# Token shift of the first two tiles moved into the projection's last chunks, and the leading tile's identity products taken out, in a hybrid RWKV-7 and latent-attention encoder step

## What is computed

```python
def _project(xn, shift_prev, w_in, mu_shift):
    p = jnp.einsum('bld,dc->blc', xn, w_in)
    pr, pm = p[..., :C_RWKV], p[..., C_RWKV:]
    prev = jnp.concatenate([shift_prev.astype(pr.dtype), pr[:, :-1]], axis=1)
    return pr + mu_shift * (prev - pr), pm, pr[:, -1:]
```

## Time and profile before

| | us |
|---|---|
| median of three runs | 2065.2 (2061.5 to 2069.67) |
| the profiled execution | 2070.0 |
| its span, first to last instruction | 2067.8 |
| projection, to the last copy by ACT | 308.9 |
| first instructions of the mixing of the prompt | 311.5 |
| PE busy in the span | 1895.7 |
| mean granted PE clock | 0.949 |

### The profile page before, as it was taken

The page is one execution under the profiler, slowest core; times in us unless marked ns, Lnnn a source line. Parts: engine busy times, 40 slices in busy tenths (PEclk is TensorE's granted clock), DMA queues, the critical chain, the costliest instruction groups (busy, mean ns, idle before and its releaser), DMA issues. The chain is left out here.

```text
span 2067.8 us, 39290 instructions
## 1 busy us (share of the span) xinstructions
PE 1895.7 (92%) x16543; PEld 1621.1 (78%) x16543; DVE 934.5 (45%) x1810; ACT 670.2 (32%) x1318; POOL 356.3 (17%) x330
## 2 busy tenths in 40 slices
PE   6999995888898898898877999999999999999997
PEld 6999993666666666666665888999999999899996
DVE  7610105455666655655425365333354333543335
ACT  2221211234344444444323113333343333333332
POOL 0000004322322221221110041300003100032100
PEclk9999996779999999999788999999999999999999
DMA  6452111101210110100133514444434444444441
GB/s 223 139 202 68 65 44 54 47 5 45 77 40 21 58 58 2 57 33 26 52 99 135 193 52 121 129 126 122 126 119 151 138 127 122 123 142 141 127 128 61
DMA packets 167889, 196.28 MB, mean 95 GB/s; under 512 B 18786, under 2 KB 142458, under 8 KB 166580
## 3 DMA queue, kind: packets, MB, share of 16 engines
q1 hardware_dynamic: 165556, 186.35, 28.7%
q0 software_dynamic: 2192, 7.93, 1.0%
HBM read 165.82 MB, written 29.25 MB: 94 GB/s over the span
## 5 line engine op out<-in xcount | busy, mean ns | idle before, releaser
L675 DVE TENSOR_TENSOR c_wo_lo<-c_raw,c_wo_hi 128x1024 fp32r<-128x1024 f32 x94 | 115.2, 1225 | 454.9 <-ACT c_wo_hi L602 454.7
L821 PE MATMUL c_pY<-c_wo_hi,c_hl 128*128 128x512 f32 x564 | 221.3, 392 | 0.0
L821 PE MATMUL c_pY<-c_wo_lo,c_hh 128*128 128x512 f32 x564 | 221.0, 392 | 0.0
L821 PE MATMUL c_pY<-c_wo_hi,c_hh 128*128 128x512 f32 x564 | 220.5, 391 | 0.0
L602 ACT ACTIVATE c_wo_hi<-c_raw 128x1024 fp32r<-128x1024 f32 x94 | 99.7, 1061 | 325.0 <-PE c_pY L821 325.0
L562 POOL TENSOR_TENSOR c_hid<-c_relu 128x384 f32<-128x384 f32 x96 | 79.3, 826 | 669.7 <-ACT c_relu L617 669.7
L853 PE MATMUL c_pU<-c_zT_hi,c_wo_hi 128*128 128x384 f32 x768 | 151.3, 338 | 1.7 <-DVE c_zT_lo L670 1.6
L853 PE MATMUL c_pU<-c_zT_lo,c_wo_hi 128*128 128x384 f32 x768 | 148.6, 334 | 0.0
L853 PE MATMUL c_pU<-c_zT_hi,c_wo_lo 128*128 128x384 f32 x768 | 148.5, 334 | 0.0
L853 PEld LDWEIGHTS c_pU<-c_zT_hi,c_wo_hi 128*128 128x128 f32 x768 | 137.7, 188 | 10.2 <-DVE c_zT_lo L670 2.7
L853 PEld LDWEIGHTS c_pU<-c_zT_hi,c_wo_lo 128*128 128x128 f32 x768 | 134.5, 188 | 0.0
(11 more groups left out here) (463 smaller groups left out, 3444.8 us busy)
## 6 DMA issues: line engine op xcount, KB each, us to landing
c_raw<-w_down SPq DMA_DIRECT2D x96, 512.0 KB, 3.6
c_raw<-w_up SPq DMA_DIRECT2D x96, 512.0 KB, 4.7
scratch_p<-a_o SPq DMA_DIRECT2D x72, 154.0 KB, 1.8
a_w<-w_in SPq DMA_DIRECT2D x8, 1232.0 KB, 8.3
m_prev<-scratch_p SPq DMA_DIRECT2D x8, 896.0 KB, 4.6
m_pr<-scratch_p SPq DMA_DIRECT2D x5, 1232.0 KB, 5.3
b_pr<-scratch_p SPq DMA_DIRECT2D x4, 1232.0 KB, 5.3
scratch_h<-a_x POOLq DMA_DIRECT2D x9, 512.0 KB, 4.5
```

The lines of the kernel that those rows point to most:

```text
L675: dve.tensor_tensor(row_lo[slot_of(U)], row_raw[U % 2][:, :], row_hi[slot_of(U)].bitcast(F32), ALU.subtract).then_inc(S("row_lo"), 1)
L821: last = pe.matmul(pY[2 * t + half][:, :], x, w[:, 512 * half:512 * half + 512], start=first and a == 0, stop=final and a == 2, skip_group ...
```

## The change

1. In the projection's last pair the SP loads, as soon as chunk 5 is stored in full, the first 1792 columns of tile 0 and of the rows one earlier, and some six tiles later those of tile 1. DVE, behind its last `w_low`, does the shift of both tiles in three operations each. Chunk 7 takes the meta tile and tile 1 first, and SP then loads their other 672 columns. To hold the rows across the barrier, `w_raw` is laid over the two `pr` buffers, and the input ring with `ln_in_g` and `ln_in_b` becomes a tensor `ring` that later phases use for other buffers.
2. `shift_diff` and `shift` of tiles 0 and 1 are gone from the mixing, with the loads of `pr` and `prev` for them and the waits on them. SP no longer waits for tile 0's transposes before it loads tile 1's table.
3. The constants that DVE sets move from the head of the phase to tile 0's `latent_keys`, POOL's two clears to its `lora_up`, behind `key_squares`.
4. All seven groups of identity products in tile 0 are gone.

```diff
-        x = [sb(f"a_x{i}", [P, D]) for i in range(RING)]
-        g_row, b_row = sb("a_g", [P, D]), sb("a_b", [P, D])
+        x = [M["ring"][:, i, :] for i in range(RING)]
+        g_row, b_row = M["ring"][:, 4, :], M["ring"][:, 5, :]
+
+        rows_early = [M["pr0"], M["pr"]]
+        past_early = [M["ring"][:, 2 * i:2 * i + 2, :].rearrange("p a d -> p (a d)") for i in range(EARLY)]
...
-        w_raw = [sb(f"a_w{i}", [P, KD, CH]) for i in range(2)]
+        w_raw = [rows_early[i][:, :].rearrange("p (k n) -> p k n", k=KD) for i in range(2)]
...
+        def tiles_of(half, more):
+
+            return list(range(NW)) if more or half == 0 else [NW - 1] + list(range(NW - 1))
...
+                    for m, w in enumerate(tiles_of(half, more)):
+                        if not more and (half, m) in ((0, 0), (1, EARLY)):
+                            for slot in range(4):
+                                sp.wait_ge(S(f"p_stored{slot}"), 16 * ((c + half) * NW + m) // 4)
+                        if not more and (half, m) == (0, 0):
+                            load_shifted(0)
+                        if not more and (half, m) == (0, 6):
+                            load_shifted(1)
+                        if not more and (half, m) == (1, EARLY):
+                            for i in range(EARLY):
+                                t0, n = TILES[i]
+                                sp.dma_start(rows_early[i][0:n, C_RWKV:C_IN], io["p"][1 + t0:1 + t0 + n, C_RWKV:C_IN])\
+                                  .then_inc(S("rest_landed"), 16)
+                        store_p((c + half) * NW + m, c + half, (NW * half + m) % 4, w)
+
+            def load_shifted(i):
+
+                t0, n = TILES[i]
+                if i == 0:
+                    sp.wait_ge(S("h_transposed"), 2 * NW)
+                    for s in range(RING):
+                        sp.wait_ge(S(f"h_stored{s}"), 16 * len(range(s, NW, RING)))
+                sp.wait_ge(S("w_lo"), N_CH - 1 + i)
+                sp.dma_start(rows_early[i][0:n, 0:C_RWKV], io["p"][1 + t0:1 + t0 + n, 0:C_RWKV])\
+                  .then_inc(S(f"early_landed{i}"), 16)
+                sp.dma_start(past_early[i][0:n, 0:C_RWKV], io["p"][t0:t0 + n, 0:C_RWKV]).then_inc(S(f"early_landed{i}"), 16)
...
+            dve.wait_ge(S("weights_landed"), 16 * len(mix_loads(io, M)))
+            for i in range(EARLY):
+                n = TILES[i][1]
+                p_, past = rows_early[i][0:n, 0:C_RWKV], past_early[i][0:n, 0:C_RWKV]
+                dve.wait_ge(S(f"early_landed{i}"), 32)
+                step(dve.tensor_tensor(past, past, p_, ALU.subtract))
+                step(dve.tensor_tensor(past, past, M["mu"][0:n, :], ALU.mult))
+                step(dve.tensor_tensor(p_, p_, past, ALU.add))
...
-    return steps
+    return [(s, i, v) for s, i, v in steps if i >= EARLY or s not in ("shift_diff", "shift")]
...
-                if i == 0 and step in ("newton_x", "scan_sa", "scan_s"):
-                    spin(pe, SC[:, 0:P], ident, ident, 12 if (step, v) == ("newton_x", 0) else 3)
...
-                    if i == 0:
-                        pe.wait_ge(S("sh_mu"), 1)
-                        spin(pe, SC[:, 0:512], ident, four_const, 3)
...
-                    if i == 0:
-                        spin(pe, SC[:, 0:P], ident, ident, 16)
...
+                if s == "lora_up" and i == 0:
+                    pool.memset(vbd[:, :], 0.0).then_inc(S("vbd_zero"), 1)
+                    pool.wait_ge(S("vbd_zero"), 1)
+                    pool.memset(kTall[QH:QH + 1, :, :], 0.0).then_inc(S("later_clear"), 1)
+                    pool.wait_ge(S("later_clear"), 1)
...
                 if s == "key_squares":
-                    pool.wait_ge(S("shifted"), i + 1)
+                    wait_shifted(pool, i)
+                    if i == 1:
+                        pool.wait_ge(S("KT_src"), 1)
+                        pool.wait_ge(S("b_ready"), 1)
...
                 if s == "decay":
+                    if i == 1:
+                        J.wait_filled(act, (0, "KT"))
+                        act.wait_ge(S("BT_src"), 1)
...
+                if s == "latent_keys" and i == 0:
+                    dve.memset(qT[QH:QH + 1, :, 0:CHUNK], -1e30).then_inc(S("first_set"), 1)
+                    dve.memset(qT[QH:QH + 1, :, CHUNK:P], 0.0).then_inc(S("first_set"), 1)
+                    for m in (CM, QM, PM):
+                        step(dve.memset(m, 0.0))
+                    for m in (IA, X0):
+                        for ck in range(2):
+                            R = rows_of(P, ck)
+                            step(dve.tensor_copy(m[R, :, :], ident[R, R].unsqueeze(1).to_broadcast([CHUNK, HEADS, CHUNK])))
+                    dve.memset(state[:, :, :], 0.0).then_inc(S("state_ready"), 1)
```

More of the change, by code:

```diff
@@ L101 @@
 N_CH = C_IN // CH
+EARLY = 2
 ORDER = list(range(1, LAST + 1)) + [0]
@@ L254, in pair @@
                 for half in range(2):
-                    for w in range(NW):
-                        u = NW * half + w
-                        drain((c + half) * NW + w, u % 4, w, c * 4 * NW + 16 * (u // 4))
-                        if w == 1 and (half == 0 or more):
+                    for m, w in enumerate(tiles_of(half, more)):
+                        u = NW * half + m
+                        drain((c + half) * NW + m, u % 4, w, c * 4 * NW + 16 * (u // 4))
+                        if m == 1 and (half == 0 or more):
                             w_high(c + half + 1, 1 - half)
@@ L363, in project, with pair @@
                 last.then_inc(S("p_filled"), 1)
-            def pair(c):
+            def pair(c, more):
                 for half in range(2):
                     pe.wait_ge(S("w_lo"), c + half + 1)
-                    for w in range(NW):
-                        pe.wait_ge(S("p_drained"), (c + half) * NW + w - 3)
-                        project((NW * half + w) % 4, half, w)
+                    for m, w in enumerate(tiles_of(half, more)):
+                        pe.wait_ge(S("p_drained"), (c + half) * NW + m - 3)
+                        project((NW * half + m) % 4, half, w)
             pe.wait_ge(S("ident_landed"), 16)
@@ L386, in _ @@
             with pe.Fori(1, N_CH // 2 - 1) as j:
-                pair(2 * j)
-            pair(N_CH - 2)
+                pair(2 * j, True)
+            pair(N_CH - 2, False)
 BLK = 3
```

75 lines of the change are left out of this document (35 added, 40 removed).

## The result

| | before | after |
|---|---|---|
| median of the runs taken together, us | 2064.69 (4 runs, 2061.5 to 2069.67) | 2037.13 (4 runs, 2033.83 to 2038.1) |
| the profiled execution | 2070.0 | 2037.2 |
| its span | 2067.8 | 2035.4 |
| PE busy in the span | 1895.7 | 1879.3 |
| mean granted PE clock | 0.949 | 0.950 |

The ratio is 0.9861, 95% interval 0.9842 to 0.9879: 27.6 us faster, where 26.4 were forecast.

What follows compares the result with a forecast made beforehand. It took PE to bound the projection and a chain beside PE the mixing's first 22 us. 16.5 − 3.5 + 5.4 + 2.4 + 1.8 + 3.6 + 1.0 − 0.8 = 26.4 us, giving 2039; range 2031 to 2047.

Steps and rivals of the forecast that it cites:

- both of tile 1: Tile 1's shift leaving the mixing gains 3.6 us; its norm, no longer held beside POOL's key product, gains 1.0.
- the constants: Constants and clears inside tile 0's chain hold the key norm and delay the key copy: 3.5 us lost, bounds 0 and 4.6.
- identity products: Removing tile 0's groups gains 5.4 us in the Gram products, 2.4 before the first X, 1.8 in later steps.
- What bounds: PE bounds the projection; a chain beside PE (constants, shift, norm) bounds the first 22 us of the mixing.
- that case, with 2.7: If the rotation table lands some 1.5 us earlier, POOL's clear ends earlier and the constants lose 2.7 us.
- the last: Three products each ahead of the third X product, scan_sa and scan_s: removal gains 1.8 us, bounds 0 and 5.0.
- The first rival: The clock stays low through tile 1's wide products, up to 11.5 us more, 2050; 12 in 100.
- The term of 0.8: Lower granted clock without the identity products: 0.8 us lost, bounds a gain of 1 and a loss of 6.
- Given back: The start's gain is lost to something the shift hid, such as a longer load: 2051 to 2057; 6 in 100.
- slower: SP's waits and loads in the projection make PE stand still over 26 us, ending above 2065.2; 3 in 100.
- More: No hold, an early table, all identity groups worth full time: 35.8 us gained, 2029 to 2031; 7 in 100.

Runs made afterwards that it cites:

- e9: The changed kernel with 8 more DVE subtractions of 128x1792 behind the early shift in the projection; median 2048.25 us, ratio to before 0.9883.
- e10: The changed kernel with 24 more DVE subtractions of 128x1792 behind the early shift in the projection; median 2054.36 us, ratio to before 0.9914.
- e6: The changed kernel with POOL's clear of the key tile's last row moved behind tile 1's key product; median 2041.19 us, ratio to before 0.9869.
- e2: The changed kernel with all seven groups of identity products back at their old places; median 2048.95 us, ratio to before 0.9885.
- e8: The changed kernel with POOL's clear and DVE's memsets moved, and identity products added while PE awaits tile 0's latent row; 2039.35 us, ratio 0.9868.

## Why the prediction was right

The forecast was 2039, and 2037.1 and 2043.9 were measured, 27.6 and 23.5 us less than before on the same chips. The mechanism is borne out by the terms: four of eight, among them both of tile 1, came out within 0.1 us. That the sum fell within 0.3 us is luck: the constants gave 2.0 us more than forecast, and three other terms 1.7 less. And two terms that look right hide errors of their own, as told under identity products.

- **What bounds.** The start was a chain beside PE; e9 shows that the work moved into the projection is free, and e10 that its cover is DVE's idle time up to the barrier.
- **The constants** were mis-sized, −3.5 against −1.5. The mechanism was right: the clear holds a one-input `TENSOR_SCALAR` until its own end (e6: 0.16 without it). The rule of the Trainium skill, page "SBUF — State Buffer", section "Who interferes with whom", said that the clear, which reads nothing, would block such an operation and not a two-input one; the trace agrees with both: L1855 at 2.25 us, and L1839, with two tensor inputs beside the same clear, at 0.47 as before. What was off is the moment: the table landed 1.5 us after its issue and not 3.6, so the clear ended at 323.47 instead of 325.6, and the block of constants ended 2 us sooner. The prediction named that case, with 2.7; the rest is that the latent row, from which this term counts, came 0.5 later than put. So the copy stood at 333.93, where PE's products at half clock would have released it at 332.5; e6 gets 1.3 us back by moving the clear.
- **Identity products**: 9.6 forecast, 8.3 between the traces of before and after, 9.2 by putting them back. The step that was wrong is the last, and not by its 1.8 being too high: the three places cost 3.0 (e2), each 1.65 us of products of which 0.7 to 1.1 reached the chain. The prediction took the clock of before there to be the lower level, from the stretch of 385.3 to 392.0; but right ahead of it, from 381.9 to 385.3, PE ran at 0.99. That is 2.2 us of clock that the changed kernel lacks and the sum does not have, so that only 0.8 is left to see.
- **The clock.** The first rival is refuted: tile 1's key, value and query products ran at 1.00 from 366.6 to 378.0, though the stretch ahead of them, 350.5 to 364.0, was at 0.50 with PE busy 12.32 of 13.5. The term of 0.8 was mis-sized: the loss is 0.8 in the Newton step and 2.2 in tile 0's last steps, 3.0 in all, inside the stated bound of 6. The Newton step's clock came with the identity products (e2 has 1.00 from 347.5 to 352.0 again); that of the last steps isn't shown to, since e2 with the same products ran there at 0.50. That the products bought little holds for the places where they stood; e8 shows that it isn't general, since such products ahead of tile 0's wide ones brought full clock there, for 10 us, which the chain had no use for.
- **Given back, slower**: PE was busy for 73.5 of 73.5 us from 235 to 308.5, with both loads and the shift in it, and the phase started 0.5 us later.
- **More** (2029 to 2031) needed the table early and no hold. The table came early; the hold stayed.

What stays open, beside the 3 to 5 us of e10: which execution gets which clock in the later tiles and just ahead of tile 1's scores. Identical instructions ran at 0.87 and at 0.83 of the clock in the same stretch, and I made no experiment on that.

## What to carry to other kernels

Work of a serial start that hangs on nothing but stored results belongs under the matrix work of the phase ahead, and its price is zero until that engine's idle time up to the barrier is used up, then every microsecond. Sum such a change link by link along the chain and not by busy times: two things that hide each other (here tile 1's shift and the identity products, which up to the second `T` copy were worth 3.4 us alone in the old kernel and 6.2 in the new) aren't additive. Where a change of 1 to 5 us is to be judged and times scatter with the granted clock by 10, compare distances in the trace, from one instruction to the next, and keep whole times for what is larger. Compare the granted clock of the same stretch too: here it moved a distance by 1.4 us between two kernels whose instructions there were the same.

## What the runs showed of the hardware

- A write-only clear on POOL (7.03 us, one partition, 8320 elements) stretched a DVE `TENSOR_SCALAR` of 16x8 from 0.16 to 2.25 us, to 20 ns past its own end.
- Two-input operations aren't free of POOL: L76, a `SCALAR_TENSOR_TENSOR` of 16x2, took 1.14 us instead of 0.15 beside POOL's two-input product, and ended 0.02 after it.
- The granted clock fell to 0.50 while PE was busy all the time (e8, 327 to 330), and stayed there from 317 to 364 in the changed kernel, though PE was busy all of the time from 321 to 335; it rose from 364 on (0.82, then 1.00), in the last of tile 1's decay products.
- The same sixteen products of tile 1 took 3.43 us at 0.50 in after and 1.93 us in e9, whose chain is the same up to there.
- One program's executions spread over 30 us with a mean clock from 0.933 to 0.952.
